# The projection phase of a hybrid mLSTM and pooling block: raw weight loads moved from the sync engine's DMA queue to ScalarE's, and stage loads in pairs

## The reference

```python
parts_x = _split_proj((_rmsnorm(x, norm_w) * (1 + scale) + shift) @ in_w)       # q k v o z_m gates p z_p g_branch
parts_c = _split_proj((_rmsnorm(xc, norm_w) * (1 + scale_c) + shift_c) @ in_w)  # context: only k, v, q, gates used
h_c, st_f, st_b = _bi_mlstm(qc, kc, vc, lic, lfc, zero, zero)                   # scan over the context, both directions
h_x, _, _ = _bi_mlstm(qx, kx, vx, lix, lfx, st_f, st_b)                         # scan over the latent tokens
y_m = _mlstm_branch(h_x, parts_x, head_norm_w, branch_m_w)                      # norm, * sigmoid(o) * silu(z_m), projection
y_p = _pool_branch(parts_x, (rows, GRID_W), (1, 2), pool_w, pool_scale, branch_p_w)
x = x + gate * (sigmoid(g_m) * y_m + sigmoid(g_p) * y_p) @ out_w                # then a final rmsnorm
```

## Time and profile before

| what | us |
|---|---|
| median of three runs | 2519.4 (2517.57 to 2523.01) |
| the profiled execution, its own time | 2528.66 |
| its span in the trace | 2526.8 |
| projection phase in the trace, 144 to 971 | 827 |
| TensorE busy in that phase | 744.31 |
| VectorE, GpSimd, ScalarE busy in that phase | 435.18, 290.75, 254.13 |

### The profile page before, as it was taken

How to read it: one execution, slowest core, us unless ns; L and a number is a source line. 1 busy time by engine, 2 the same in 40 slices (tenths; PEclk the granted TensorE clock), 3 DMA queues, 4 the chain that set the end, 5 groups by cost and what they waited for, 6 DMA issues and landing times. The chain is left out here.

```text
span 2526.8 us, 35639 instructions
## 1 busy us (share of the span) xinstructions
PE 2329.2 (92%) x12515; PEld 1980.7 (78%) x12515; DVE 1459.5 (58%) x2655; ACT 954.9 (38%) x1938; POOL 581.2 (23%) x489
## 2 busy tenths in 40 slices
PE   7789998977888998999999999999999689999998
PEld 4668787866666786888888888888888578797878
DVE  1644554555465554657576756676666355656564
ACT  2633232333232333344444434444444344343532
POOL 0032342332433422212122211222121112121210
PEclk9799999998999998999999999999999799999999
DMA  9496876688577767667667687766666555666663
GB/s 287 155 258 125 164 168 163 164 227 151 116 144 129 202 171 242 204 233 232 204 225 248 214 303 239 248 209 213 215 220 227 177 151 187 207 199 204 197 207 111
DMA packets 405410, 501.67 MB, mean 199 GB/s; under 512 B 24264, under 2 KB 290036, under 8 KB 399732
## 3 DMA queue, kind: packets, MB, share of 16 engines
q1 hardware_dynamic: 387396, 421.80, 56.1%
q0 software_dynamic: 7712, 35.65, 6.5%
q10 hardware_dynamic: 10128, 41.95, 4.7%
HBM read 352.82 MB, written 163.27 MB: 204 GB/s over the span
## 5 line engine op out<-in xcount | busy, mean ns | idle before, releaser
L1741 PE MATMUL bank<-xlate,wh 128*128 128x512 f32 x2048 | 672.0, 402 | 14.9 <-DVE v_t L1875 10.5
L1741 PEld LDWEIGHTS bank<-xlate,wh 128*128 128x128 f32 x2048 | 374.2, 190 | 84.4 <-DVE v_t L1875 10.7
L1741 PE MATMUL bank<-xlate,wl 128*128 128x512 f32 x1024 | 410.3, 401 | 0.0
L1041 PE MATMUL bank<-xlate,wh 128*128 128x512 f32 x1024 | 341.7, 409 | 38.6 <-DVE wl L1219 36.0
L1041 PE MATMUL bank<-xtop,wh 128*128 128x512 f32 x768 | 250.6, 403 | 23.1 <-DVE wl L1219 12.5
L1041 PEld LDWEIGHTS bank<-xlate,wh 128*128 128x128 f32 x1024 | 197.2, 196 | 84.9 <-issue 36.8
L1741 PEld LDWEIGHTS bank<-xlate,wl 128*128 128x128 f32 x1024 | 194.0, 189 | 34.3
L1041 PE MATMUL bank<-xlate,wl 128*128 128x512 f32 x512 | 206.6, 404 | 0.0
L1234 DVE SCALAR_TENSOR_TENSOR tmp<-bank,psum 128x512 f32<-128x512 f32 x128 | 88.2, 689 | 195.3 <-PE bank L1041 83.4
L1041 PEld LDWEIGHTS bank<-xtop,wh 128*128 128x128 f32 x768 | 144.4, 193 | 55.2 <-ACT wh L1072 24.0
L1898 DVE SCALAR_TENSOR_TENSOR state<-state,cols,bank 128x516 f32<-128x516 f32 x128 | 95.8, 748 | 112.8 <-PE bank L1702 112.6
(11 more groups left out here) (305 smaller groups left out, 5250.2 us busy)
## 6 DMA issues: line engine op xcount, KB each, us to landing
v_t<-vk_d SPq DMA_DIRECT2D x144, 384.0 KB, 3.9
qk_d<-os SPq DMA_DIRECT2D x32, 1024.0 KB, 5.7
q_t<-qk_d SPq DMA_DIRECT2D x128, 256.0 KB, 4.2
wraw<-wpair_d ACTq DMA_DIRECT2D x31, 1024.0 KB, 6.7
rawb<-in_in_w_dram SPq DMA_DIRECT2D x32, 512.0 KB, 11.2
vk_d<-os SPq DMA_DIRECT2D x16, 1024.0 KB, 4.8
wpair_d<-in_in_w_dram POOLq DMA_DIRECT2D x16, 1024.0 KB, 15.7
k_t<-qk_d SPq DMA_DIRECT2D x64, 256.0 KB, 4.6
```

The costliest lines, as they stand in the source:

```text
L1041: mm = pe.matmul(dst[:, :], a[:, kd, :], x_block(part, XB[name])[:, kd], start=(kd == 0 and n == 0), stop=(kd == KH - 1 and n == 2))
L1741: mm = pe.matmul(bank[m % 2][:, :], a[:, u % 2, k, :], xlate[part][:, BLOCK_OF[k // KH, tq], k % KH], start=(k == 0 and n == 0), stop=(k = ...
```

## The change

1. `raw_in` moves from SP's program to ScalarE's, so that the raw weights go by queue q10. Unit 1 is asked for at the start of the block. Unit u + 1 is asked for at the step p with POS[p + 3] = (u, M1), right after the `split_hi` of that position, behind a wait for the low part of M3 of unit u - 1.
2. The load of the first weight pair of the next phase (`wpair`, 1 MB) moves in the same way.
3. `block_in` loads two neighbouring channel tiles with one request of 512 KB; it waits for both buffers, and one semaphore counts both. There are 16 requests in place of 32. A pair is asked for one position after its second tile's buffer has been used.

```diff
             @block.sync
-                def raw_in(u):
-                    ...
-                raw_in(1)
...
-                    if p < NPOS and POS[p][1] == "M4" and POS[p][0] + 2 < NU:
-                        u = POS[p][0] + 2
-                        sp.wait_ge(op_lo, AT[u - 2, "M3"] + 1)
-                        raw_in(u)
-                    if p == AT[NU - 1, "M1"]:
-                        sp.wait_ge(op_lo, AT[NU - 2, "M3"] + 1)
-                        sp.dma_start(wpair, in_v[:, :, O0:O0 + 2 * P]).then_inc(pair_loaded, 16)
             @block.scalar
+                def raw_in(u):
+                    half, i, kind = UNITS[u]
+                    dst = raw_of(u)
+                    if kind == "s":
+                        for n, c0 in enumerate((POOL0 + i * P, ZP0 + i * P)):
+                            act.dma_start(dst[:, :, n * P:(n + 1) * P], in_v[:, :, c0:c0 + P]).then_inc(raw_loaded[u % 2], 16)
+                    else:
+                        c0 = {"q": Q0, "k": K0, "v": V0}[kind] + i * HD
+                        for n in range(2):
+                            act.dma_start(dst[:, KH * n:KH * (n + 1), :], in_v[:, KH * n:KH * (n + 1), c0:c0 + HD])\
+                                .then_inc(raw_loaded[u % 2], 16)
                 def block_in(n):
                     if n >= NST:
-                        act.wait_ge(rb_lo, n - NST + 1)
-                    act.dma_start(stage[:, n % NST], xr_d[RB[n // KH][2], n % KH]).then_inc(st_loaded[n % NST], 16)
+                        act.wait_ge(rb_lo, n - NST + 2)
+                    act.dma_start(stage[:, n % NST:n % NST + 2],
+                                  xr_d[RB[n // KH][2], n % KH:n % KH + 2].rearrange("k p t -> p k t")).then_inc(st_loaded[n % NST // 2], 16)
...
+                raw_in(1)
                 for n, w in enumerate((CTX, TQ, TQ)):
                     split_hi(n)
...
                     if p + 3 < NPOS:
                         split_hi(p + 3)
+                        u, name = POS[p + 3]
+                        if name == "M1" and 1 <= u < NU - 1:
+                            act.wait_ge(op_lo, AT[u - 1, "M3"] + 1)
+                            raw_in(u + 1)
+                        if name == "M6" and u == NU - 1:
+                            act.wait_ge(op_lo, AT[NU - 2, "M3"] + 1)
+                            act.dma_start(wpair, in_v[:, :, O0:O0 + 2 * P]).then_inc(pair_loaded, 16)
...
-                    for n in range(NST, NRB):
-                        if RB_AT[n - NST] + 1 == p:
+                    for n in range(NST, NRB, 2):
+                        if RB_AT[n + 1 - NST] + 1 == p:
                             block_in(n)
```

More of the change, by code:

```diff
@@ L633, in hybrid_block @@
             tm_stored = [sem2(f"tm_stored{n}") for n in range(NTM)]
-            st_loaded = [sem2(f"st_loaded{n}") for n in range(NST)]
+            st_loaded = [sem2(f"st_loaded{n}") for n in range(NST // 2)]
             rb_hi = sem2("rb_hi"); rb_lo = sem2("rb_lo")
@@ L1178, in _ @@
                         act.wait_ge(prod_done, LAST_CTX + 1)
-                        for n in range(NST):
+                        for n in range(0, NST, 2):
                             block_in(n)
@@ L1185, in _ @@
                         act.wait_ge(cols_st, 32)
-                        for n in range(NRB, NRB + KH):
+                        for n in range(NRB, NRB + KH, 2):
                             block_in(n)
@@ L1194, in _ @@
                             act.wait_ge(prod_done, AT[UA if n < NRB else NU - 1, RB[n // KH][0]] + 1)
-                            act.wait_ge(st_loaded[n % NST], 16 * (n // NST + 1))
+                            act.wait_ge(st_loaded[n % NST // 2], 16 * (n // NST + 1))
                             act.activation(x_block(0, b)[:, kd], stage[:, n % NST], ACT.Copy).then_inc(rb_hi, 1)
-                    for n in range(NST, NRB):
-                        if RB_AT[n - NST] + 1 == p:
+                    for n in range(NST, NRB, 2):
+                        if RB_AT[n + 1 - NST] + 1 == p:
                             block_in(n)
```

## The result

| | us |
|---|---|
| before, median of 4 runs | 2521.2 (2517.6 to 2523.0) |
| after, median of 4 runs | 2552.3 (2547.1 to 2554.7) |
| ratio | 1.0122, 95% interval 1.0101 to 1.0144 |
| profiled execution of after | 2547.06, span 2545.3 |

The prediction said 2506, and 2484 to 2528 as the range. The loss lies where the diff is. From the phase's end to the span's end both profiles take 1556 us (2545.3 - 989.6 and 2526.8 - 971.2; the two ends are those of a 10.5 us wait of TensorE at the start of the next phase). The phase itself is 18.4 us longer. That is less than the 31 us between the medians: the profiled execution of before was 7 us over its median and that of after 5 us under its own.

The account below looks back on a forecast made before the run. TensorE, 92% busy, was taken as the bound, so only its idle or slow time could be won. The terms, -16.2 - 3 + 2 + 2 + 1 + 1 = -13 us off the 2519.4 median, gave 2506; range 2484 to 2528.

Parts of the forecast that it names:

- What bounds the kernel: Projection phase: TensorE waits 30.8 us outside the switch for VectorE's `wl`, held up by late stores to `zp_d`.
- The store passes raw weights by its own queue (-16.2 us): Five `wl` gaps outside the switch: stores take turns with raw weights and land sooner, winning 16.2 of 30.8 us.
- a rival: Descriptors are made in order whoever asks, so stores land with raw weights as before and gaps stay: 2515 to 2524, chance 0.17.
- Stores in competition (+2 and +1): Stores formerly ahead of raw weights now take turns: 2 us worse at the 625 us gap, 1 us for later v stores.
- The slower rival: ScalarE, asking for unit 17's raw weights in the switch under a copy, stops over 10 us more: 2530, chance 0.19.
- +1 for the switch: Switch: tiles share q10 with unit 17's raw weights; between 10 us worse and 6 better, taken as 1 us worse.
- +2 for ScalarE's stops: Projection phase: raw-weight requests stop ScalarE; about 10 us is covered, TensorE waits for the excess, taken as 2 us.
- The clock (-3): After long gaps TensorE runs at half clock; with four of five gaps shortened and one or two gone, 3 us won.
- The remark on alignment: Alignment of GpSimd's 16 copies with the `s` units shifts with every microsecond won before; named as a way to fail, unsized.

Follow-up runs that it names:

- the best version: Kernel before, SyncE asking for raw weights in quarters at four steps, and copies inside the DRAM in quarters three products apart: 2461.1 us, ratio 0.9755.
- the run of other columns: Changed kernel with unit 7 reading the key weights of head 2 in place of head 1: 2549.7 us, ratio 1.0081.
- the run with unit 7 later: Changed kernel with only unit 7's raw weights asked for two products later: 2536.4 us, ratio 1.0051.
- three more pairings: ScalarE against SyncE asking: halves without copies 2494.8 and 2483.3 us; quarters with whole copies 2516.5 and 2508.8; quarters with quartered copies 2470.2 and 2461.1.
- the copies shifted: All 16 copies inside the DRAM asked for four products later: changed kernel 2522.5 us, ratio 1.0011; kernel before 2500.8, 0.9913.
- the pair without copies: Kernels before and after without the 16 copies inside the DRAM, scan phase reading pairs from the input: 2483.3 us (0.9838) and 2494.8 (0.9892).

## Why the prediction was wrong

**What bounds the kernel: right.** `wl` waits behind VectorE's L1234 behind a store; shorter landings did remove them (17.5 us left of 48.5 in the best version).

**The store passes raw weights by its own queue (-16.2 us): the step that failed.** It measured 4.7 us: outside the switch the waits on `wl` went from 30.8 to 26.1 us. I took the one-for-one turns of rows 9 as a promise of eight turns. The `zp_d` stores of the gaps landed 14.6 us (asked for at 432.4) and 18.2 us (781.9) after asking, as against 15.7 and 16.5:

```profile
L819 SPq DMA_DIRECT2D zp_d<-tmp x2: 320/326/332, 781.9 to 804.8; - x2
...
DMA to landing us min/median/max: 2.3/10.2/18.2
```

With raw weights under way stores took 8.3 us in the mean before and 8.8 after, with a copy as well 14.0 and 13.8. The tile of rows 11, which did not pass, was the right row to go by, as a rival then did at 0.17. But its reason, descriptors made in common, is not what the runs show: raw weights from GpSimd's own queue hold the stores just as long (9.5 and 15.2 us). The rule of the Trainium skill that speaks against this change, in "DMA: Bandwidth & Descriptors", section "Issuing engines are not separate DMA queues", held, in that the gain of 16.2 us did not come. The turns packet by packet of its section "Queues, rings and completion order" agree with the run of other columns (441 packets of q1 to 502 of q10) and not with the store that moved no packet for 9.4 us while q10 moved hundreds; whether the engines gave q1 no turn there or q1 had nothing ready, no run shows.

**Stores in competition (+2 and +1): the term that was mis-sized.** It measured 25 us: `os` 3.6 to 24.1 us in the profile and `wh` 9.5 to 14.4, and 16 of the 31 us in one meeting by the run with unit 7 later. I costed it as turns shared with raw weights, where in that meeting it was a place behind them. I looked at the gap at 625, where a store was late already (it went from 6.62 to 6.14 us), and priced all stores that had been in front of raw weights, such as the one of 293.9 with its landing of 5.4 us, at 3 us together; the ones hurt by the old order had each a row of their own.

**The slower rival** (ScalarE stopped in the switch, 2530) had the sign and not the mechanism. Waits on `wl` from 545 to 605 us are 20.0 us, against 17.7, and ScalarE's largest stop there is 3.09 us:

```profile
561.60 3.09 ACTq L1058 DMA_DIRECT2D rawb<-in_in_w_dram  x2
```

So +1 for the switch measured about +2. The +2 for ScalarE's stops was not measured by itself; the longest stop for raw weights is 3.8 us, and none stands just before a gap of TensorE. (In the switch 10 requests fall away, not the 12 of the prediction; nothing hangs on it.)

**The clock (-3)** fell away with the gain it hung on: 0.94 in place of 0.95 in the phase.

**The remark on alignment** with the 16 copies, which I left as a way for the sum to fail, was worth 20 to 30 us in either kernel and should have widened the range at both ends.

What stays open: of the 31 us, 16 are the one meeting. Some 8 to 12 us stay with ScalarE's asking in three more pairings, and 22 with the copies shifted. In the pair without copies the profiles put about half of it behind stores to `qk_d` and half in the switch, but no run took either away. With nothing long under way the cost is gone, which argues for the moment of asking, but that was not shown: no run moved that moment and held all other meetings fixed.

## What to carry to other kernels

A queue of its own is no promise that a store passes large loads that were asked for just before it: here stores landed no sooner with one (8.3 and 8.8 us). Cut the large ones up, by steps of the work, until one piece is shorter than the wait that a store can bear. When a request moves, list the transfers that it will now precede as well as those that it will no longer precede, and price each by its landing time with such company. And before crediting an edit in such a phase, shift an unrelated transfer by a few steps: if the time moves by 20 us, a single schedule tells little of the edit.

## What the runs showed of the hardware that was not expected

**Some columns of one tensor are read at about half the speed.** The raw weights of head 1 (256 columns each of q, k and v) came slowly. In the two kernels without copies, where least else is under way, their packets of 1 KB took 155 to 184 ns in the mean (units 4, 5, 7, 18, 26 and 27), and those of heads 0, 2 and 3 took 64 to 98. The queues of before from 797 to 805 us (v of head 1) and 443 to 449 us (k of head 3), nothing else under way:

```profile
q1 hardware_dynamic: 693, 0.69, 98.7%
...
q1 hardware_dynamic: 893, 0.90, 88.7%
```

0.987 x 16 x 8 us over 693 packets is 182 ns each; 0.887 x 16 x 6 over 893 is 95. The scan phase of the same two kernels, which reads pairs of weight blocks straight from the tensor, shows it again: of 31 pairs, the eight that hold the second 256 columns of their kind (o, z_m and the two branch gates) took 147 to 192 ns a packet, the other 23 took 47 to 97. So it is the second quarter of each of seven blocks of 1024 columns. The pieces are as long and as far apart in all cases; why these columns differ, no run shows. In the projection phase such a read is what the store of 292.82 stood behind.

**A copy inside the DRAM holds the 16 engines longest where it reads these columns.** Packets of 4 KB took 0.85 us each in the copy of the earlier trace rows (597.1 to 620.4), but that copy reads a second quarter. In the mean of a copy the four of this kind took 0.67 to 0.88 us in before, the other twelve 0.19 to 0.56; a store's packet of 2 KB took 83 ns (482 packets in 31.2% of 16 engines for 8 us, above). A store asked for while a copy was under way landed in 10 to 11.5 us in the mean. The gaps at 434.83, 625.26 and 788.97 come just after copies of the slow kind; that the slow reads cause them was not tested. In four parts, 64 requests in place of 16, the same bytes let a store land in 6.0 us.
